# Hybrid mixer and expert trunk on one core: norm statistics per token, first panels in pairs, another order at the start

## What is computed

```python
for l in range(DEPTH):                                   # 2
    mod = silu(c) @ w_mod[l] + b_mod[l]                  # 6 x 1024: sh1, sc1, g1, sh2, sc2, g2
    h = rmsnorm(x) * (1 + sc1) + sh1                     # 1st norm of the layer
    z = h @ w_in[l]                                      # then three token mixers, gates
    ...
    x = x + g1 * (merged @ w_o[l])
    h2 = rmsnorm(x) * (1 + sc2) + sh2                    # 2nd norm of the layer
    x = x + g2 * peer(h2, w_pq[l], sub_keys[l], u_tab[l], v_tab[l])
return rmsnorm(x, final_norm)
# rmsnorm(x) = x * rsqrt(mean(x*x over features) + eps)
```

## Time and profile before

| | us |
|---|---|
| median of 3 runs | 3599.91 |
| lowest and highest run | 3599.59, 7039.04 |
| profiled execution, own time | 3599.65 |
| its span, first to last instruction | 3597.9 |
| TensorE matmul busy | 3484.4 (97%) |
| VectorE busy | 2483.5 (69%) |
| ScalarE busy | 1463.0 (41%) |
| GpSimd busy | 879.9 (24%) |
| mean granted clock of TensorE | 0.988 |

### The profile page before, as it was taken

One profiled execution on the slowest core, in us unless ns is written; L12 is line 12 of the kernel. 1 busy time (PEld: TensorE's weight loads), 2 busy tenths in 40 slices (PEclk: granted clock), 3 DMA queues, 4 the chain that ended last, 5 costly groups with the idle time before them and its releaser, 6 DMA issues.

```text
span 3597.9 us, 53854 instructions
## 1 busy us (share of the span) xinstructions
PE 3484.4 (97%) x18220; PEld 2936.6 (82%) x18220; DVE 2483.5 (69%) x4639; ACT 1463.0 (41%) x2538; POOL 879.9 (24%) x1027
## 2 busy tenths in 40 slices
PE   5999999999999999999989998999999999999998
PEld 3776789999999777777767776999999997777775
DVE  6455688889888775555464566888898878655554
ACT  3334233335776333323243333333367753323322
POOL 0010100004334534444400010000053345344442
PEclk8999999999999999999999999999999999999999
DMA  7353434447999988999744433444499999899995
GB/s 258 116 190 125 149 122 148 146 150 287 355 342 340 395 326 338 358 350 346 290 148 153 161 127 120 149 150 150 147 339 345 342 359 379 300 357 352 357 349 199
DMA packets 269525, 909.67 MB, mean 253 GB/s; under 512 B 32212, under 2 KB 65028, under 8 KB 268452
## 3 DMA queue, kind: packets, MB, share of 16 engines
q0 software_dynamic: 126496, 473.44, 35.8%
q1 hardware_dynamic: 105984, 383.83, 29.8%
q10 hardware_dynamic: 36868, 50.35, 3.9%
HBM read 792.14 MB, written 115.34 MB: 252 GB/s over the span
## 4 chain that ended last, share of the span: by engine, by line
PE 92%; DVE 3%; DMA 3%; issue 1%; ACT 1%; POOL 0%; ACTq 0%; SPq 0%; DVEq 0%; POOLq 0%
PE ps L458 16%; PE ps L460 15%; PE ps L459 15%; PE ps L958 10%; PE ps L959 10%; PE ps L960 10%; PE ps L938 5%; PE ps L972 3%; PE ps L776 2%; DMA urow<-in_u_rows,idu 1%; PE ps L832 1%; DMA mod<-in_w_mod 1%; PE ps L899 1%; PE ps L873 1%; PE ps L874 1%
## 5 line engine op out<-in xcount | busy, mean ns | idle before, releaser
L458 PE MATMUL ps<-mov,whl 128*128 128x384 f32 (+1 forms) x2880 | 1042.5, 362 | 48.2 <-DVE whl L445 30.4
L460 PE MATMUL ps<-mov,whl 128*128 128x384 f32 (+1 forms) x2880 | 1014.8, 352 | 0.0
L459 PE MATMUL ps<-mov,whl 128*128 128x384 f32 (+1 forms) x2880 | 1012.2, 351 | 0.0
L445 DVE TENSOR_TENSOR whl<-raw,whl 128x1024 fp32r<-128x1024 f32 x648 | 793.3, 1224 | 205.1 <-ACT whl L435 188.1
L435 ACT CAST whl<-raw 128x1024 fp32r<-128x1024 f32 x648 | 680.0, 1050 | 107.3 <-ACT hst L1148 74.8
L958 PE MATMUL ps<-whl,wgthl 128*128 128x512 f32 x1536 | 614.3, 400 | 14.9 <-DVE wgthl L1646 14.8
L458 PEld LDWEIGHTS ps<-mov,whl 128*128 128x128 f32 x2880 | 543.0, 189 | 102.9 <-issue 38.5
L959 PE MATMUL ps<-whl,wgthl 128*128 128x512 f32 x1536 | 610.6, 398 | 0.0
L960 PE MATMUL ps<-whl,wgthl 128*128 128x512 f32 x1536 | 610.1, 397 | 0.0
L667 POOL DMA_INDIRECT urow<-in_u_rows,idu x256 | 304.5, 1189 | 1225.7 <-DVE idu L1579 787.3
L460 PEld LDWEIGHTS ps<-mov,whl 128*128 128x128 f32 x2880 | 542.3, 188 | 35.3
(11 more groups left out here) (245 smaller groups left out, 3453.9 us busy)
## 6 DMA issues: line engine op xcount, KB each, us to landing
raw<-in_uT_tab SPq DMA_DIRECT2D x256, 512.0 KB
raw<-in_v_tab SPq DMA_DIRECT2D x256, 512.0 KB
expert_spill<-hst ACTq DMA_DIRECT2D x256, 192.0 KB
hin<-expert_spill POOLq DMA_DIRECT2D x256, 192.0 KB
gt<-weight_spill POOLq DMA_DIRECT2D x64, 768.0 KB
weight_spill<-stage POOLq DMA_DIRECT2D x22, 2048.0 KB
raw<-in_w_in SPq DMA_DIRECT2D x72, 512.0 KB
raw<-in_w_mod SPq DMA_DIRECT2D x64, 512.0 KB
```

What stands on the lines that cost most here:

```text
L445: nc.vector.tensor_tensor(whl[:, m % RING, 1], raw[:, raw_n(m) % RAW], whl[:, m % RING, 0].bitcast(F32), ALU.subtract).then_inc(lo_done, 1)
L458: nc.tensor.matmul(o, w[:, 0, k], src[:, 0, k, :cols], start=(k == 0), stop=False)
L459: nc.tensor.matmul(o, w[:, 0, k], src[:, 1, k, :cols], start=False, stop=False)
L460: mm = nc.tensor.matmul(o, w[:, 1, k], src[:, 0, k, :cols], start=False, stop=(k == KC - 1))
```

## The change

- The sums of squares of the norms over x are made the other way round: the squares (128 features x 128 tokens) are the stationary operand, one column of ones moves (`token_squares`), and the sum of a token stands on the token's partition, 128x4 in all. Root and reciprocal work on 128x4. `spread_root` puts the result back on all partitions: four matmuls with a column of the reciprocal, broadcast, as the stationary operand and the identity as 128 moving columns. VectorE reads it from PSUM. The norms inside the attention's latents stay as they were.
- `gemm_two`: the first two panels behind a norm over x run side by side, six products for each chunk. It waits for both panels' low parts first.
- The squares of a layer's first norm stand at the end of TensorE's loop over the layers (for layer 0 ahead of it). The first pair of heads is written out ahead of the loop over pairs.
- `warm_root` makes ScalarE take a root of a 128x1 tile ahead of the squares.
- The start: x is SP's first transfer, 8 buffers for the panels of w_mod, shift and scale panels in turn. VectorE makes 12 of the 16 columns, then the norm's first two chunks, then the other four columns between the chunks; low parts of panels 0 and 1 behind the scalings; the angles behind all that.
- At the boundary panel 0 is split ahead of the norm, and the bias of layer 1 is added during layer 0's last stage.

The diff, cut to its core:

```diff
+MOD0 = 8
...
+BIAS_AT = P - 16
...
+    def gemm_two(pe, l, m, rows):
+        for j in range(2):
+            pe.wait_ge(lo_done, 1 + l * M_ALL + m + j + 1)
+            pe.wait_ge(bank_free[(m + j) % 2], 1 + l * N_BANKED + (m + j) // 2)
+        for k in range(KC):
+            pe.wait_ge(rows[0], rows[1] + k + 1)
+            for j in range(2):
+                w, o = whl[:, (m + j) % RING], ps[:, (m + j) % 2]
+                nc.tensor.matmul(o, w[:, 0, k], mov[:, 0, k], start=(k == 0), stop=False)
+                nc.tensor.matmul(o, w[:, 0, k], mov[:, 1, k], start=False, stop=False)
+                mm = nc.tensor.matmul(o, w[:, 1, k], mov[:, 0, k], start=False, stop=(k == KC - 1))
...
+    def token_squares(pe, tile, bank, first, last):
+        for t in range(TT):
+            mm = nc.tensor.matmul(ps[:, bank, t:t + 1], tile[:, t * P:(t + 1) * P], ones[:, 0:1], start=first and t == 0,
+                                  stop=last and t == TT - 1)
+        return mm
+
+    def spread_root(pe, bank, n, count):
+        pe.wait_ge(rstd_ready, n)
+        for t in range(TT):
+            mm = nc.tensor.matmul(ps[:, bank, t * P:(t + 1) * P], rinv4[:, t:t + 1].to_broadcast([P, P]), ident[:],
+                                  start=True, stop=True)
+        mm.then_inc(root_spread, 1)
+
+    def first_squares(pe, l):
+        for q in range(KC):
+            if q == 0:
+                pe.wait_ge(x_added, l * KC + 3)
+            pe.wait_ge(sq_ready, l * SQ_ALL + SQ_H1 + q + 1)
+            token_squares(pe, sq[:, q % 2], 2, q == 0, q == KC - 1).then_inc(sq_used, 1)
+
+    def rstd4(dve, l, k):
+        dve.wait_ge(root_ready, l * 4 + k + 1)
+        nc.vector.reciprocal(rinv4[:], rt4[:]).then_inc(rstd_ready, 1)
...
+        if k in (0, 3):
+            nc.scalar.activation(rt4[:], ps[:, SSQ_BANK[k], :TT], ACT.Sqrt, bias=eps[:], scale=1.0 / width
+                                 ).then_inc(root_ready, 1)
...
+    def warm_root(act):
+        nc.scalar.activation(warm[:], eps[:], ACT.Sqrt)
...
+        sp.dma_start(x_sb[:], xT).then_inc(x_in, 16)
         for i in range(MOD_FIRST):
-            if i >= 4:
-                sp.wait_ge(mod0_done, i - 3)
-            sp.dma_start(mod0[:, i % 4], w_mod[i]).then_inc(mod0_in[i % 4], 16)
-            if i == 3:
+            if i >= MOD0:
+                sp.wait_ge(mod0_done, i - MOD0 + 1)
+            sp.dma_start(mod0[:, i % MOD0], w_mod[i % 2 * KC + i // 2]).then_inc(mod0_in[i % MOD0], 16)
+            if i == MOD0 - 1:
...
+        first_squares(pe, 0)
+        spread_root(pe, 2, 1, 1)
         with pe.Fori(0, DEPTH) as l:
-            for q in range(KC):
-                if q == 0:
-                    pe.wait_ge(x_added, l * KC + 3)
-                sum_squares(pe, l, SQ_H1 + q, 2, q == 0, q == KC - 1)
...
+                elif kind == "panel" and i == 0:
+                    gemm_two(pe, l, 0, (mov_ready, l * 3 * KC))
...
-            nc.tensor.matmul(ps[:, 2], ones[:], root[:], start=True, stop=False)
-            sum_squares(pe, l, SQ_H2 + KC - 1, 2, False, True)
+            token_squares(pe, root, 2, True, False)
+            pe.wait_ge(sq_ready, l * SQ_ALL + SQ_ALL)
+            token_squares(pe, sq[:, (SQ_ALL - 1) % 2], 2, False, True).then_inc(sq_used, 1)
+            spread_root(pe, 2, l * 4 + 4, l * 2 + 2)
...
+            two_heads(0, first=True)
+            settle(pe)
+            with pe.Fori(1, PH // 2) as two:
+                two_heads(two)
...
+            first_squares(pe, l + 1)
+            pe.wait_ge(x_added, l * KC + 2 * KC)
+            spread_root(pe, 2, l * 4 + 5, l * 2 + 3)
...
+                warm_root(act)
+                if l:
+                    split_hi(act, l, 0)
...
         def first_columns(start, stop):
+            for c in range(start, stop):
+                for i in (2 * c, 2 * c + 1):
+                    dve.wait_ge(mod0_in[i % MOD0], 16 * (i // MOD0 + 1))
+                    at = i % 2 * KC + c
+                    mod_column(mod[:, at:at + 1], mod0[:, i % MOD0], mod0_done)
...
         def norm_h(l, which):
-            rstd(dve, l, 3 * which)
-            dve.wait_ge(rstd_ready, l * 4 + 3 * which + 1)
+            if l and not which:
+                split_lo(dve, l, 0)
+            if not (l or which):
+                first_columns(0, KC - 2)
+            rstd4(dve, l, 3 * which)
+            dve.wait_ge(root_spread, l * 2 + which + 1)
             sh, sc = (0, 3 * KC)[which], (KC, 4 * KC)[which]
             for c in range(KC + 1):
+                if not (l or which) and c in (2, 4):
+                    first_columns(KC - 3 + c // 2, KC - 2 + c // 2)
...
-                if not which and c in (1, KC):
-                    split_lo(dve, l, c // KC)
+                if not (l or which) and c >= KC - 1:
+                    split_lo(dve, l, c - (KC - 1))
+                if l and not which and c == 1:
+                    split_lo(dve, l, 1)
...
             norm_h(l, 0)
+            if l == 0:
+                angles()
```

More of the change, by code:

```diff
@@ L184, with __init__, link @@
 class Chain:
[L188 to L195, removed]
+    def __init__(self, eng, sem):
+        self.eng, self.sem, self.n = eng, sem, 0
+    def link(self, ins):
         ins.then_inc(self.sem, 1)
         self.n += 1
[L199 to L216, removed]
+        self.eng.wait_ge(self.sem, self.n)
 def build_trunk(nc, xT, c, pos, freq, bands, w_mod, b_mod, w_in, w_sT, b_s, qkv_gain, w_uq, w_ukv,
-                w_pool, pool_scale, w_abc, w_o, w_pq, keysT, uT_tab, u_rows, v_tab, fin_gain, out, dve_chain):
+                w_pool, pool_scale, w_abc, w_o, w_pq, keysT, uT_tab, u_rows, v_tab, fin_gain, out):
     gate_d = nc.dram_tensor("gate_spill", [3 * KC, P, S], F32, kind="Internal").ap()
@@ L889, in _ @@
                     m = M_T + n
-                    gemm(pe, l, m, more=two * (2 * (2 + T_U)), more_half=two * (2 + T_U),
-                         rows=None if n else (mov_ready, l * 3 * KC + 2 * KC), cols=S if j < 2 else SD)
+                    if first and n == 0:
+                        gemm_two(pe, l, m, (mov_ready, l * 3 * KC + 2 * KC))
+                    elif not first or n > 1:
+                        gemm(pe, l, m, more=two * (2 * (2 + T_U)), more_half=two * (2 + T_U), cols=S if j < 2 else SD)
                     if j in (2, 3):
@@ L1035, in norm_h @@
             take_root(act, l, 3 * which, D)
-            if not which:
-                for m in range(LEAD):
-                    split_hi(act, l, m)
+            if l and not which:
+                split_hi(act, l, 1)
             sh = (0, 3 * KC)[which]
@@ L1043, in norm_h @@
                                      ).then_inc(t_hi, 1)
+                if not (l or which) and c >= KC - 3 and c < KC - 1:
+                    split_hi(act, l, c - (KC - 3))
         for l in range(DEPTH):
-            act.wait_ge(consts_made, 2)
             norm_h(l, 0)
+            if l == 0:
+                act.wait_ge(rope_made, 1)
+                nc.scalar.activation(sin[:], ang[:], ACT.Sin)
+                nc.scalar.activation(cos[:], over[:], ACT.Sin).then_inc(rope_made, 1)
             for kind, i in STEPS:
@@ L1237, in _ @@
     def _(dve):
[L1238 removed]
+        chain = Chain(dve, dve_step)
         dve.wait_ge(c_ready, 1)
@@ L1253, in _ @@
-        setup.link(last)
-        magic, tau = 12582912.0, 2 * np.pi
-        parts = [6.28125, 0.0019340515136718750]
-        parts.append(tau - sum(parts))
-        setup.link(nc.vector.tensor_scalar(turns[:], ang[:], 1.0 / tau, magic, ALU.mult, ALU.add))
-        setup.link(nc.vector.tensor_scalar(turns[:], turns[:], magic, None, ALU.subtract))
-        for part in parts:
-            setup.link(nc.vector.scalar_tensor_tensor(ang[:], turns[:], -part, ang[:], ALU.mult, ALU.add))
-        below = float(np.nextafter(np.float32(np.pi), np.float32(0)))
```

125 lines of the change are left out of this document (67 added, 58 removed).

## The result

Before 3599.75 us median (4 runs), after 3572.51 us (4 runs, 3571.57 to 3573.02); the ratio is 0.9924, 95% interval 0.9912 to 0.9935. One run of before was disturbed (7039.04) and is left out of the ratio.

What follows compares the result with a forecast made beforehand. TensorE, busy 97% of the span, was taken as the bound, with only five pauses movable. Start +1.5, second norms -9.3, boundary -3.7 and end +1.2 gave -10.3 on 3599.65, hence 3589.3 us; range over the cases 3573 to 3597.

Steps and rivals of the forecast that it cites:

- five places: Start, both layers' second norms, layer boundary and last norm: TensorE's pauses, said to be all the change can move.
- Passes and second norm of layer 0: One-column passes 0.11 us apart; second norm: H 2.5 us earlier, pair of panels 13.3 us, together -4.65.
- H: Moment at which VectorE starts to scale a norm's first chunk; forecast 2.5 us earlier in second norms.
- Second norm of layer 1: Same term as in layer 0: H 2.5 us earlier, pair gains 2.6, together -4.65.
- E: Moment at which the second panel behind a norm is done; forecast H + 15.6 for H + 18.18 in second norms.
- Boundary: Between the layers: squares 1.94 us earlier, smaller root and reciprocal, pair gains 2.7, clock's fall costs 3.4; -3.7.
- End: Last norm: root, reciprocal and spreading less squares give -2.2 us, clock's fall costs 3.4; +1.2.
- Start: Program start: loads at 390 GB/s give H = 30.0, but a longer way to the products, E = 63.1; +1.5 us.
- The clock did not hold: Rival, 0.25: one-column passes count as work, pairs run at full clock; 3576.6 us.
- neither 0.055 nor 0.22: Pass spacings in us of two rivals: 0.055 cheap (0.08, 3572.8), 0.22 slower, weight loads in series or half clock (0.10, 3602.8).
- the loads did come sooner: Rival at the start, 0.05: loads don't come sooner, buffers were not what held them; +5.5 instead of +1.5, 3593.4.
- Cheap passes: Rival, 0.08: passes 0.055 us apart, ScalarE's square and handoffs pace the chunks, done before the clock falls; 3572.8.

Runs made afterwards that it cites:

- e1: Kernel before with one unused tile of 96 bytes a partition behind eps, nothing else of the change: 3577.19 us, ratio 0.9935.
- e8: Changed kernel with the second four gathers of v_tab rows and the next modulation panel's load three panels later: 3566.70 us, ratio 0.9906.
- e3: Kernel before with only wgthl and the two tiles behind it moved by 32 bytes, wgthl to 180992: 3591.88 us, ratio 0.9978.
- e4: Kernel before with 64 unused bytes behind eps, wgthl at 181024: 3598.79 us, ratio 0.9995.
- e6: Kernel before with 32 unused bytes behind eps, wgthl at 180992: 3590.58 us, ratio 0.9974.
- e7: Kernel before with only wgthl and the two tiles behind it moved by 96 bytes, wgthl to 181056: 3579.89 us, ratio 0.9944.
- e2: Changed kernel with 32 bytes more behind eps, wgthl at 181088: 3590.95 us, ratio 0.9974.
- e9: e8 with 64 unused bytes behind eps, wgthl at 181120, a multiple of 256 bytes from whl: 3551.95 us, ratio 0.9863.
- e11: Changed kernel with the first two panels behind a norm one after the other, as before: 3576.65 us, ratio 0.9936.
- e5: Separate kernel of matmuls alone, 288 of 512 columns for each of 20 address pairs, reference left out: 226.7 to 234.3 ns apart.
- e10: e9 with unread 512-column matmuls in TensorE's pauses among squares, ahead of and behind the spreading, at boundary, end and second norms: 3553.88 us.
- e13: e9 with unread 512-column matmuls behind the spreading alone, 6 in each second norm, 7 at the boundary: 3546.12 us, ratio 0.9853.

## Why the prediction was wrong

The step that failed is the one on which all others stood: "These five places are all the change can move; between them TensorE hardly ever waits, and every stage starts from the one before, so what is gained there shifts the rest." I counted waits and took the pace of matmuls as given. It was a property of two addresses, and the three small tiles that the diff adds changed one of them. By e1 that is -21.1 us in the value stages (598.1 and 599.2 to 588.1 and 588.0). The second half of the same step failed too: between the places TensorE does wait, 1.54 and 3.36 us in the value stages, for rows behind the burst of gathers. The changed kernel's stages are 5.1 us longer than e1's, and e8 gives back 5.8. Quicker matmuls are a part of that (e1 waits 1.1 twice, before not at all); why the row took longest in the changed kernel is open. The forecast's -10.3, with -21.1 and +5.1, is -26.3; measured were -27.2. That the two are so close is partly luck: by the medians at equal spacing the rest of the change is worth 7.8 us and not 10.3.

The rest of the sum, point by point.

- *Passes and second norm of layer 0.* 0.114 us a pass at full clock for 0.11, H 3.71 behind the first sum for 3.6, a pair of 13.32 for 13.3. Right.
- *Second norm of layer 1.* The forecast has the clock fall among the squares at boundary and end only, 4.2 us or more behind the last full matmul. Here it was down 2.2 us behind w_o's last product, and of the 2.5 forecast for H 0.5 came. The pair gained 3.2 for 2.6, since the clock was also back sooner. From the first sum to E the two layers gain 4.9 and 3.75 us. The rest of the table's -6.0 and -4.6 lies behind E, in a stretch of untouched code that takes 721.2 to 724.4 us in e1, e3, e4, e6 and e7. So -4.6 for -4.65 in layer 1 is luck.
- *Boundary.* H 12.4 behind the squares for 13, pair 13.8 for 13.3, no jump exposed. The clock fell 4.6 us behind the first pass, as forecast. -4.0 for -3.7. The forecast's own terms add up to 4.1 for H and 3.5 for the clock, not 4.4 and 3.4, which makes -3.3; and the same stretch takes 36.95 to 39.72 us in the padded kernels of before (37.28 in before), and 33.29 to 33.35 in the changed kernel, e2, e8 and e9, so by kernel the gain is 3.6 to 6.4.
- *End.* +1.3 for +1.2: squares 10.36 for 7.60, and the small root and reciprocal do not make up for it. In e2, e8, e9 and e11, with the same code, the end takes 23.49 to 25.31, which is +0.1 to +1.9.
- *Start.* H at 31.05 for 30.0, first product 50.20 for 49.8, E +1.8 for +1.5. The forecast had the loads as the bound of the twelfth column. But the columns began at 13.16, when the first panel was there, and followed each other without a pause, 1.27 us apart, so from there VectorE was the bound and not the loads, which ran at 404 GB/s over the 30 us to 36 us. The 358 GB/s of the Trainium skill (DMA: Bandwidth & Descriptors, Where 436 GB/s comes from) is not what this core meets.
- *Rivals.* The clock did not hold, passes were neither 0.055 nor 0.22, the loads did come sooner. "Cheap passes" gave 3572.8, 0.3 from the median, and its mechanism is refuted: a time alone proves no story. "A stage between the five places changes its length" was on the list of what would make me wrong, and was what happened.

## What to carry to other kernels

Read the spacing of the matmuls in every long stage, not only the waits: here 5 ns in each of 4608 were more than all that the change was made of. When tiles are added, compare the addresses of the operands that come after them; a padding tile is the cheapest experiment there is. A stage that gets quicker asks for its transfers sooner, so look which of its waits had only a few us of cover left. And compare stretches over several kernels with the same code before you believe a difference of a few us: which passes run at half clock changed from kernel to kernel, and the times with it.

## What the hardware showed that I had not expected

- The spacing of matmuls of 512 columns depends on the distance of stationary and moving tile in SBUF modulo 256 bytes: 226.7 ns at 0, 228.9 at 192, 232.4 to 234.3 elsewhere (e5; steps of 32 bytes, addresses as listed). The Trainium skill (TensorE: Matmul & The Clock Gate, Step-by-step: what each phase is for) says that loading the next tile's weights does not steal read bandwidth from the running matmul, through a port of its own. These runs do not show which of the two is held up, but the two are not independent: where one tile lies relative to the other moves each matmul by up to 7.6 ns. What makes it so, and why 192 is better than its neighbours, stays open.
- At the start the record has the granted clock at 1.00, but the 64 passes are 0.213 us apart (12.57 to 26.00), as at half clock elsewhere, and the spreading takes 2.08.
- One wide matmul in every 1.1 us among one-column passes did not keep the clock up (e10, down at 1783.80); six or seven in a row behind them, in a pause, brought it back sooner (e13: 1.00 again 3.4 us behind H in the second norms, 6.2 and 7.6 in e9).
